# Differential attention: the logits of a head's first two query tiles in one step, with two reorderings beside it

## The reference, cut to what matters

```
s1 = einsum('bqhd,bkhd->bhqk', a1, k1) * scale      # q tile i sees keys 0 .. 128*(i+1)-1,
s2 = einsum('bqhd,bkhd->bhqk', a2, k2) * scale      # the last 64-wide chunk masked by rows
p1 = softmax(where(mask, s1, -inf)); p2 = softmax(where(mask, s2, -inf))
p  = p1 - lam * p2
o  = einsum('bhqk,bkhe->bqhe', p, v)
o  = rmsnorm(o, b_subln, 1e-5) * (1 - lam_init)     # over the 128 columns of a head
x  = x + einsum('bse,ed->bsd', concat([o, memory_attention]), w_o)
```

## Time and profile before

| | before |
|---|---|
| median of 3 runs | 1757.56 us (1757.56 to 1759.45) |
| the profiled execution | 1758.98 us |
| its span on the core | 1757.2 us |
| PE busy | 1716.0 us, 98% of the span |
| DVE busy | 1256.5 us, 72% |
| ACT busy | 818.7 us, 47% |
| granted TensorE clock | 0.995 of full speed |

### The profile page before, as it was taken

The page is one execution under the profiler, slowest core; times in us unless marked ns, Lnnn a source line. Parts: engine busy times, 40 slices in busy tenths (PEclk is TensorE's granted clock), DMA queues, the critical chain, the costliest instruction groups (busy, mean ns, idle before and its releaser), DMA issues.

```text
span 1757.2 us, 21518 instructions
## 1 busy us (share of the span) xinstructions
PE 1716.0 (98%) x8215; PEld 1413.4 (80%) x8215; DVE 1256.5 (72%) x1915; ACT 818.7 (47%) x1345; POOL 37.8 (2%) x87
## 2 busy tenths in 40 slices
PE   8999999999999999999999999999999999999998
PEld 7887888888888777778888888788888788888886
DVE  6666358687888667765778788889987645765766
ACT  7433244343445656764433443542767532333342
POOL 0000000000001121000000000000000000000000
PEclk9999999999999999999999999999999999999999
DMA  7222442333412211116142423033100353234212
GB/s 251 84 73 84 129 135 76 117 97 107 136 45 62 64 49 61 48 49 192 48 144 71 134 72 120 12 98 106 49 13 13 90 174 96 72 92 141 66 49 84
DMA packets 195749, 158.29 MB, mean 90 GB/s; under 512 B 5248, under 2 KB 161280, under 8 KB 195648
## 3 DMA queue, kind: packets, MB, share of 16 engines
q1 hardware_dynamic: 194240, 154.16, 29.1%
q0 software_dynamic: 400, 1.25, 0.3%
q10 hardware_dynamic: 1008, 1.53, 0.2%
HBM read 154.81 MB, written 2.10 MB: 89 GB/s over the span
## 4 chain that ended last, share of the span: by engine, by line
PE 89%; DVE 6%; ACT 3%; issue 1%; DMA 0%; POOL 0%; DVEq 0%; SPq 0%; ACTq 0%
PE ps L1061 28%; PE ps L1063 28%; PE ps L1062 28%; PE ps L1565 1%; PE ps L1131 1%; ACT sb L2021 1%; DVE sb L2238 1%; ACT sb L1764 1%; PE ps L1454 0%; DVE sb L2236 0%; DVE sb L2495 0%; DVE sb L2264 0%; PE ps L1190 0%; DVE sb L2737 0%; ACT sb L1770 0%
## 5 line engine op out<-in xcount | busy, mean ns | idle before, releaser
L1061 PE MATMUL ps<-sb,sb 128*128 128x512 f32 (+3 forms) x2435 | 927.6, 387 | 9.7 <-ACT sb L2021 5.2
L1063 PE MATMUL ps<-sb,sb 128*128 128x512 f32 (+3 forms) x2435 | 911.6, 379 | 0.0
L1062 PE MATMUL ps<-sb,sb 128*128 128x512 f32 (+3 forms) x2435 | 910.9, 379 | 0.0
L2238 DVE TENSOR_TENSOR sb<-sb,sb 128x1024 fp32r<-128x1024 f32 (+1 forms) x414 | 404.8, 997 | 219.0 <-ACT sb L1764 218.2
L1061 PEld LDWEIGHTS ps<-sb,sb 128*128 128x128 f32 (+1 forms) x2435 | 450.8, 188 | 110.2 <-issue 11.9
L1764 ACT ACTIVATE sb<-sb 128x1024 fp32r<-128x1024 f32 (+1 forms) x414 | 349.7, 871 | 394.3 <-PE ps L1063 389.1
L1063 PEld LDWEIGHTS ps<-sb,sb 128*128 128x128 f32 (+1 forms) x2435 | 450.4, 188 | 86.6
L1062 PEld LDWEIGHTS ps<-sb,sb 128*128 128x128 f32 (+1 forms) x2435 | 451.1, 188 | 81.8 <-issue 0.2
L2478 DVE TENSOR_TENSOR sb<-sb,sb 128x1024 fp32r<-128x1024 f32 x70 | 85.5, 1222 | 47.5 <-ACT sb L1926 45.2
L1921 ACT ACTIVATE sb<-sb 128x512 f32<-128x512 f32 x64 | 40.3, 631 | 130.8 <-DVE sb L2530 130.8
L2460 DVE TENSOR_TENSOR sb<-sb,sb 128x1024 f32<-128x1024 f32 x80 | 95.1, 1217 | 0.6
(11 more groups left out here) (217 smaller groups left out, 1107.2 us busy)
## 6 DMA issues: line engine op xcount, KB each, us to landing
sb<-in_w_up SPq DMA_DIRECT2D x86, 512.0 KB, 4.1
sb<-in_w_down SPq DMA_DIRECT2D x86, 512.0 KB, 4.8
sb<-in_w_gate SPq DMA_DIRECT2D x22, 512.0 KB, 3.9
sb<-in_a_w_in SPq DMA_DIRECT2D x20, 512.0 KB, 3.8
sb<-in_w_in SPq DMA_DIRECT2D x20, 512.0 KB, 3.7
sb<-in_w_o SPq DMA_DIRECT2D x16, 512.0 KB, 3.7
sb<-in_w_mem_kv SPq DMA_DIRECT2D x8, 512.0 KB, 7.5
sb<-in_w_out SPq DMA_DIRECT2D x8, 512.0 KB, 3.8
```

The lines of the kernel that those rows point to most:

```text
L1061: mm(ps, lh, rh, start=start, stop=False, **k)
L1062: mm(ps, lh, rl, start=False, stop=False, **k)
L1063: return mm(ps, ll, rh, start=False, stop=stop, **k)
L2238: tt(lo, raw, hi, ALU.subtract).then_inc(S("w_lo"), parts)
```

## The change

- PE: D of tile 0 now writes the logits of tile 0 and of tile 1 behind it, in the same two banks; tile 1's 256 columns start at column 128 (`logit_columns`). The D of tile 1 is gone from PE, with its wait for the exponentials of tile 0. The sums of squares move to columns 384 to 391 of bank 0, and the wait on `rs_v` that guards them goes from tile 1's D to tile 2's.
- DVE: the maxima of tile 0 wait until both tiles' logits are there (`df_s` at u + 2), and so does the scaling of the sums of squares. The maxima of tile 1 stay in their slot, but behind the low part of the T there (the last turn of the head before), no longer ahead of it.
- ACT and DVE: R, the factors of the norm, goes ahead of X(tile 0) in slot p+1.

No instruction is added or dropped on any engine.

```
-        if s < 24:
+        if s < 24 and s % 4 != 1:
             PLAN_B[p].append(("D", s))
         if 0 <= s - 2 < 24:
             PLAN_B[p].append(("T", s - 2))
+        if s < 24 and s % 4 == 1:
+            PLAN_B[p].append(("D", s))
         if 0 <= s - 1 < 24:
             PLAN_B[p].append(("M", s - 1))
+        if s >= 8 and s % 4 == 0:
+            PLAN_B[p + 1].append(("R", s // 4 - 2))
         if s < 24:
             PLAN_B[p + 1].append(("X", s))
...
-        if s >= 8 and s % 4 == 0:
-            PLAN_B[p + 1].append(("R", s // 4 - 2))
...
+    def logit_columns(i):
+
+        at = 128 if i == 1 else 0
+        return slice(at, at + 128 * (i + 1))
...
-            elif kind == "D":
+            elif kind == "D" and a[0] % 4 != 1:
...
                 q.wait_ge(S("df_exp"), 2 * u)
...
-                if i == 1 and u >= 8:
+                if i == 2 and u >= 8:
                     q.wait_ge(S("rs_v"), USE["sub", u // 4 - 2] + 1)
...
+                unit_logits(u)
+                if i == 0:
+                    unit_logits(u + 1)
...
-                q.wait_ge(S("df_s"), u + 1)
+
+                q.wait_ge(S("df_s"), u + (2 if i == 0 else 1))
...
-                q.wait_ge(S("df_s"), 4 * a[0] + 9 if a[0] < 4 else 21 + a[0])
-                rsqrt_a(("sub",) + a, banks[B.lb][:, 256:264:2], 4, 1.0 / 128, SUBLN_EPS)
+                q.wait_ge(S("df_s"), 4 * a[0] + 10 if a[0] < 4 else 21 + a[0])
+                rsqrt_a(("sub",) + a, banks[B.lb][:, 384:392:2], 4, 1.0 / 128, SUBLN_EPS)
```

More of the change, by code:

```diff
@@ L1407, in head_sums, with unit_logits @@
             for t in range(4):
-                m = mm(banks[B.lb][:, 256 + 2 * t:258 + 2 * t], OQ1[:, 128 * t:128 * t + 128], ONES[:, 0:2], start=True,
+                m = mm(banks[B.lb][:, 384 + 2 * t:386 + 2 * t], OQ1[:, 128 * t:128 * t + 128], ONES[:, 0:2], start=True,
                        stop=True)
             return m
+        def unit_logits(u):
+            i = u % 4
+            x, h, _ = heads_of(u // 4)
+            nk, cols = 128 * (i + 1), logit_columns(i)
+            (Qh, Ql), (Kh, Kl) = QT["Q" + x], KT["K" + x]
+            q.wait_ge(S("mb_b6_lo"), B.hi["rt", "K" + x, i] + 1)
+            q.wait_ge(S("mb_b6_lo"), B.hi["rt", "Q" + x, i] + 1)
+            for w in range(2):
+                r = slice(64 * w, 64 * w + 64)
+                mm3(banks[B.lb + w][:, cols], Qh[r, h, 128 * i:128 * i + 128], Ql[r, h, 128 * i:128 * i + 128],
+                    Kh[r, h, 0:nk], Kl[r, h, 0:nk], True, False)
+            for w in range(2):
+                r = slice(64 * w, 64 * w + 64)
+                m = mm(banks[B.lb + w][:, cols.stop - 128:cols.stop], MQ[r, :], MK[r, :], start=False, stop=True)
+            m.then_inc(S("df_s"), 1)
         def unit_step(kind, *a):
@@ L1426, in unit_step @@
                 m.then_inc(S("mb_b6"), 1)
-            elif kind == "D":
+            elif kind == "D" and a[0] % 4 != 1:
                 u, i = a[0], a[0] % 4
-                x, h, _ = heads_of(u // 4)
-                nk = 128 * (i + 1)
-                (Qh, Ql), (Kh, Kl) = QT["Q" + x], KT["K" + x]
-                q.wait_ge(S("mb_b6_lo"), B.hi["rt", "K" + x, i] + 1)
-                q.wait_ge(S("mb_b6_lo"), B.hi["rt", "Q" + x, i] + 1)
                 q.wait_ge(S("mb_exp"), 16)
@@ L1439, in unit_step @@
                     head_sums(u // 4 - 2)
-                if i == 1 and u >= 8:
+                if i == 2 and u >= 8:
                     q.wait_ge(S("rs_v"), USE["sub", u // 4 - 2] + 1)
-                for w in range(2):
-                    r = slice(64 * w, 64 * w + 64)
-                    mm3(banks[B.lb + w][:, 0:nk], Qh[r, h, 128 * i:128 * i + 128], Ql[r, h, 128 * i:128 * i + 128],
-                        Kh[r, h, 0:nk], Kl[r, h, 0:nk], True, False)
-                for w in range(2):
-                    r = slice(64 * w, 64 * w + 64)
-                    m = mm(banks[B.lb + w][:, nk - 128:nk], MQ[r, :], MK[r, :], start=False, stop=True)
-                m.then_inc(S("df_s"), 1)
+                unit_logits(u)
+                if i == 0:
+                    unit_logits(u + 1)
             elif kind == "T":
@@ L2020, in unit_step @@
                 for w, E in ((0, E1[:, u % 3, 0:nk]), (1, E2[:, u % 2, 0:nk])):
-                    act(E, banks[B.lb + w][:, 0:nk], ACT.Exp, bias=M[:, 2 + w:3 + w], scale=r[:, w:w + 1],
+                    act(E, banks[B.lb + w][:, logit_columns(i)], ACT.Exp, bias=M[:, 2 + w:3 + w], scale=r[:, w:w + 1],
                         accum_out=M[:, 4 + w:5 + w]).then_inc(S("df_exp"), 1)
@@ L2637, in unit_step @@
                 for w in range(2):
-                    e.tensor_reduce(M[:, w:w + 1], banks[B.lb + w][:, 0:nk], AX.X, ALU.max).then_inc(S("df_max"), 1)
+                    e.tensor_reduce(M[:, w:w + 1], banks[B.lb + w][:, logit_columns(i)], AX.X, ALU.max).then_inc(S("df_max"), 1)
                 x, _, _ = heads_of(u // 4)
```

## The result

| | before | changed |
|---|---|---|
| median of 6 runs each | 1758.51 us (1757.51 to 1761.90) | 1763.89 us (1759.92 to 1765.38) |
| ratio, 95% interval | | 1.0020 (1.0011 to 1.0030), slower by some 3.5 us |
| span of the profiled execution | 1757.2 us | 1762.3 us |
| granted TensorE clock in it | 0.995 | 0.994 |

What follows compares the result with a forecast made beforehand. PE bounds the kernel, 89% of the chain in a 1757.2 us span, so only its waits pay. Four heads at +0.94 us give +3.8, the won 5.2 included; added to the 1757.56 median: 1761.4 us, range 1755.4 to 1763.4.

Steps and rivals of the forecast that it cites:

- Step 1: PE, turn of unit 11: 0.55 of the 1.19 us wait is won, the rest becomes a wait for DVE's combination.
- Step 2: ACT, norm factors ahead of unit 12's exponentials: high part, low part and N come earlier, still 0.49 us won.
- Step 3: DVE, maxima of unit 13 behind the low part: its exponentials start 0.94 us later, reciprocals and norm product follow.
- Step 4: PE, turn of unit 12 and the head's first piece: all gain gone, piece waits for POOL, +0.94 us; units 20 to 23 alike.
- Step 5: Other two heads, units 8 to 11 and 16 to 19: full DVE queue delays logits of units 11 and 19, +0.94 each.
- The sum: All four heads of units 8 to 23: 4 x 0.94 = +3.8 us, the won 5.2 already included.
- (a): Rival, decided at the turn of unit 11: four waits go, nothing replaces them, -5.2 us, 1752.4 us; chance 0.08.
- (b): Rival, four heads: the 0.49 us gain stays as delayed maxima find a gap, -2.0 us, 1755.6 us; chance 0.11.
- (c): Rival: only the two heads whose output a piece waits for lose, +1.9 us, 1759.5 us; chance 0.19.
- (d): Rival, whole kernel: all moved work is hidden, so the time stays at 1757.6 us; chance 0.05.
- (e): Rival: full 1.29 us in each head plus 0.63 at the maxima, up to +7 us, 1764.6 us; chance 0.05.
- 1.2 to 1.4 us later against the turn of unit 10: Trace sign on DVE: maxima of units 13 and 21 that much later against turns of units 10 or 18 than unmoved order.

Runs made afterwards that it cites:

- b3: The kernel before with only DVE's maxima of tile 1 put behind the low part of the last turn; median 1763.95 us, ratio 1.0026.
- the first run: The changed kernel with DVE's maxima of tile 1 put back ahead of the last turn's low part; median 1758.89 us, ratio 0.9997.

## Why the prediction held, and where it didn't

It said slower, by 3.8 us, through four equal delays, to 1761.4 us (1755.4 to 1763.4). Measured are 3.25 in the stretch and 3.5 (1.9 to 5.3) in the whole time; the median of 1763.89 lies 0.5 above the range. So the delay and its way are right, and the time that it was added to was not the one of this series.

The steps can be laid over the trace. The turn of unit 10, from which the walk counted, was put at 724.63 and stands at 725.66, so 1.03 comes off every time:

| | predicted | measured less 1.03 |
|---|---|---|
| turn of unit 11 on PE | 727.2 | 727.26 |
| exponentials of unit 12 | 727.10 | 727.08 |
| N on PE | 729.35 | 729.32 |
| maxima of unit 13 | 729.21 | 729.18 |
| exponentials of unit 13 | 730.19 | 730.16 |
| norm product | 731.80 | 731.78 |
| turn of unit 12 | 732.6 | 732.59 |
| second group of the piece | 734.64 | 734.60 |

**Step 1** held for units 11, 15 and 19: the wait for the exponentials became one of 0.67 for the combination, the very figure of the earlier trace rows. It did not for unit 7: the prediction looked for four such turns, and the first waits 1.56 us for the last split of the keys instead, so that of the 1.66 removed there 0.10 is won, against 0.52 in the second head. **Step 2** held in its times; the run without the moved factors shows that this part neither costs nor brings anything here. **Step 3** held, and two runs (maxima back, maxima alone) show it as the cause. **Step 4** held: waits of 0.31 for the norm product and 0.98 for POOL, twice. **Step 5**, where I had the least to go by, held as well:

```profile
718.63 0.50 PE L1068 MATMUL ps<-sb,sb 64*128 64x512 f32 x2 [0.68 <-ACT sb L2034]
...
756.83 0.51 PE L1068 MATMUL ps<-sb,sb 64*128 64x512 f32 x2 [0.66 <-ACT sb L2034]
```

**The sum was too large by 0.5.** From the start of the stretch to the turns of units 9, 13, 17 and 21 the changed kernel is later by 0.94, 1.69, 2.53 and 3.25: 0.94, 0.75, 0.84 and 0.72 a head, where the sum has 0.94 each. The mis-sized term is the 0.63 that the logits of tile 1 take in their new place. Between unit 12's mask and the turn of unit 10 they take 0.48, since their first matmul starts 0.03 behind the mask (725.02, 725.05), where the turn started 0.17 behind it before:

```profile
723.83 0.24 PE L1448 MATMUL ps<-sb,sb 64*128 64x128 bf16 x2
724.00 0.55 PE L1454 MATMUL ps<-sb,sb 128*128 128x128 f32 x3
```

0.15 a head in the three heads behind the first makes most of the missing 0.5. In the first head the logits take 0.48 as well, and the 0.94 comes out only because the rest is larger there (0.46, against 0.24 to 0.36 in the others); that this head agrees to the hundredth is luck. What to write down for a step that is moved is what it takes in the new place, not in the old, where its neighbours were others.

**Units 0 to 7** cost nothing that can be seen, as said: the stretch starts at 699.97, at 699.27 in the run with the factors back, which has the same merging, and at 699.73 before.

**The rivals.** (a), the aim met, fell at the place named, the combination; with that moved and the norm product too, 2.2 of its 5.2 us come (80.32 against 82.54). (b) needed a gap for the maxima; b3 shows that there is none. (c), only the two heads of the pieces, falls with the logits of units 11 and 19. (d) and (e) fall with the sum. The price of (e) was added up wrongly: 4 x 1.29 + 4 x 0.63 is 7.7, not 7, which would be 1765.2.

**One sign was misread.** "1.2 to 1.4 us later against the turn of unit 10" mixes two clocks. By the walk itself the maxima of unit 13 move by 1.29 (727.92 to 729.21), but the turn moves by 0.63 of that. Against the turn they are 0.63 later than before (4.55 us behind it in place of 3.92), and 0.76 later than in the first run, which has them ahead of the low part (3.79).

**The banks.** That the two tiles' logits share two banks, against the rule cited in the prediction (the Trainium skill, Perfetto Trace Analysis, Optimizing Tensor Performance), added nothing, as I had assumed: the scaling, not the maxima, was last ahead of the turn of unit 11, and DVE even waits for ACT between the maxima of unit 12 and the next low part. No run has them in separate banks, so whether that would help stays open.

**What was not foreseen at all** is how much the clock moves a median of six runs: the point of 1761.4 lies 2.5 below the median of 1763.89, and the range's end of 1763.4 just below it, while the runs of before in the same series lay 0.95 over the median that I started from. Behind 1250 us the profiled run of the changed kernel has a stretch at a lower clock that the run with the factors back has not, though both come there from the same wait of 1.8 us and 0.67 us apart, as they were 0.70 apart at the start of the stretch. The stretch's row of the changed kernel, and that of the run with the factors back; the clock is the third figure from the end:

```profile
1250.00:1260.00 10.00, 8.18 (x33) 6.30 (x32) 9.93 (x15) 9.00 (x12) 0.00 (x0) 0.83 0.30 106
```

```profile
1250.00:1260.00 10.00, 8.19 (x42) 6.51 (x40) 9.93 (x14) 9.31 (x13) 0.00 (x0) 1.00 0.34 106
```

The work of these 10 us is not touched by the change. What decides which execution meets the lower clock there, none of these runs tells.

## What to carry to other kernels

When a wait of the full engine is removed by moving work forward, look at what the other engines' in-order queues do between the old wait and the next hand-over: a step put ahead of another there delays all that is queued behind it, needed or not, and the late one may be needed several steps on (here maxima, exponentials, reciprocals, norm product, POOL, piece). First look for steps whose inputs are long there and that only stand behind others, the combination and the norm product here; moving these two, with the logits of tile 1 unmerged behind the turn, gave 0.3%, where the merging gave a loss of 0.2%. And a plan that all engines read moves a step on all of them: say for each engine what an edit moves before expecting anything of it.

## What the runs showed of the hardware

**TensorE's clock after a long wait.** In the run with the factors ahead, a wait of 1.99 us was followed by matmuls of 0.63 us at the lower level (granted 0.51), in the run with the split earlier a wait of 2.17 us likewise; waits of 1.56 and 1.66 us in the same place were followed by matmuls of 0.39 us. After the wait of 1.8 us at 1250 us one kernel fell and another didn't. So a wait that grows a little can cost more than its growth: in the run with the factors ahead 1.3 us of longer waits became 2.46 (5.2 to 6.5 us of waits, 82.54 to 85.00 us of stretch).

**DVE and POOL on the same memory.** The weight split of 128x512, which reads two operands in SBUF, took 1.36 us in place of 0.68 where it started 0.47 us into POOL's subtraction, and ended 0.55 after that one's end (735.97 against 735.42); in the changed kernel a small instruction of 0.16 us took 0.46 and ended with POOL's (735.59 against 735.58):

```profile
735.13 0.46 DVE L2656 SCALAR_TENSOR_TENSOR sb<-sb,sb 128x2 f32<-128x2 f32 x1
```

The maxima that read PSUM beside POOL kept their 1.02 us. The Trainium skill, SBUF — State Buffer, SBUF: two separate sides, says that such an instruction of VectorE with two operands in SBUF and one of GpSimd that reads SBUF exclude each other for a whole instruction. The weight split and the 128x2 instruction agree with it. The 128x8 instruction of the section on the result, which reads one operand in SBUF, was held in the same way when it started 0.01 us behind POOL's.
